# Splitting fp32 values without a mask, with five weight blocks lowered by GpSimd, in a fused two-part model on one core

## The chip, the cores and the metric

The program runs on one core of a Trainium2 chip, in one launch. The metric is the time of the whole program on the device in microseconds. The kernel before was run three times. The profile describes one further execution, of which it gives the span. Engine names are those of the profile: PE is TensorE (PEld its weight loads), DVE is VectorE, ACT is ScalarE, POOL is GpSimd, SP is SyncE, which issues the weight transfers.

## The reference

A sequence of 512 tokens of width 1024 goes through two parts. The first is two layers of this form:

```python
h = rms_norm(x, attn_norm) @ w_in            # 7 full weight blocks and a small one
h = concat(mla(6 heads), diff(6 heads), chunk(4 heads))   # softmax attention
x = x + (out_norms(h) @ w_out)               # 4 weight blocks
h = conv_ffn: rms_norm(x) @ w_ffn_in (1024 x 5632), 3-tap causal convolution over tokens,
x = x + (silu(g) * u) @ w_ffn_out (2816 x 1024)
```

The second part is one layer in which a state-space path (16 groups of states, a complex linear recurrence over the 512 tokens) and a gated attention of its own are mixed, followed by a mixture of 32 experts. All values are float32 and the products are needed nearly at float32 accuracy.

## The kernel before

**Products in three passes.** Activations lie transposed, 128 rows of the model width by 512 tokens to a tile, eight tiles `h[:, k, :]`. TensorE multiplies fp32r operands, which hold fewer bits of the fraction than float32. Each factor is therefore split into a high part in fp32r and a low part, the rest, and a product is three matmuls added into one PSUM bank: high by high, low by high, high by low (L934 to L936 in the two layers, L1178 to L1180 or L1210 to L1212 in the middle stage of the second part, "mid stage" below).

**How a value is split.** In three steps on two engines. DVE masks away the last 12 bits of the fraction (L2190 for weights, L2207 for tiles of `h`, L2502 for weights of the second part). DVE subtracts the masked copy from the source, which gives the low part (L2193, L2210, L2507), and signals `w_lowered` or `h_lowered`. ACT copies the masked part to fp32r (L1686, L1798, L1831, L1901, L1913) and signals `w_split` or `h_split`, on which PE waits.

**Weights** come in blocks of 128 x 2048 words, by one queue of SP, into a ring of three slots (`ring`). The low part of a block is written to `w_low` of its slot, its high part to one of two buffers (`w_high`, `mid_high` in the mid stage).

**Norms.** Before each projection, DVE multiplies tile after tile by the gain and the root (L2217; L2391 after attention), and each finished tile is split at once, one tile behind. ACT computes the root (L1665, L1667). The first PLAIN = 4 matmuls of the accumulation use unsplit values (L954), to give PE something to do before the first split tile is there.

**Attention** is a list of 64 blocks t (diff 0 to 23, chunk 24 to 39, latent "mla" 40 to 63; eight blocks to a pair of heads). For each t, PE makes scores, DVE adds the mask and takes the minimum (an instruction of its own, at L2332 in the kernel after), ACT takes the exponential with its sum (L1765), PE transposes, ACT copies (L1754), PE multiplies with the values. Each engine walks the list in an order written out by hand, each by its own lag.

**The mid stage.** Sixteen state groups st are processed in eight pairs. In pair p PE does, in this order: the input products B (L1241) of its two st, after `z_ready`, the scans of the pair before; a tile of an ordinary projection (128 columns of weights by 512 tokens); the output products C (L1226) of the pair before, after `rotated`; two more tiles. Per st, DVE makes six elementwise operations (L2569 to L2577) and two scans (L2581, `z_ready`), then POOL does four multiplications of 128 x 512 by powers from memory (L1584 to L1587, `rotated`) and loads the next powers (L1572). The projection tiles are `MID_TILES`, two to a weight block b, 15 blocks:

```python
MID_OF_PAIR = [range(0, 2)] + [range(3 * p - 1, min(3 * p + 2, FIRST_QK)) for p in range(1, ST // 2)]
```

ACT copies each finished tile out (L1909, L1926, L1929) and, after every odd tile i, converts block (i + 3) // 2 (L1901). DVE masks and lowers a block between the scans of one st and the elementwise operations of the next.

Of the kernel before, what the change touches and what calls it, by code (L numbers as in the profile page):

```python
# [28 lines left out]
P = 128  # L29
# [18 lines left out]
HIGH_BITS = -(1 << 12)  # L48
# [92 lines left out]
assert 13 + 2 * SMALL.index(("uq", MLA_H - 1)) < FIRST_MLA - 4 and TOKEN_BLOCKS * NQ < 13  # L141

# [144 lines left out]
REST_SPLIT = MID_SPLIT + MID_BLOCKS  # L287
RING0 = LAYERS * LAYER_BLOCKS // RING * 16
# [104 lines left out]
def build(nc, a, out):  # L393
    with ExitStack() as ctx:
# [50 lines left out]
        w_part = [extra[:, 6 * T + n * SLOT:6 * T + (n + 1) * SLOT] for n in range(2)]  # L445
# [9 lines left out]
        h_part = work[:, H_HIGH_AT * T:(H_HIGH_AT + KD) * T].rearrange("p (k t) -> p k t", k=KD)  # L455
# [35 lines left out]
        wf_part = sb("wf_part", [P, 2, KD * FH])  # L491
# [9 lines left out]
        act_part = [work[:, (JF + 6 + n) * T:(JF + 7 + n) * T] for n in range(IN_WORK)] + [spare[:, n, :] for n in range(CH_H)]  # L501
        act_part += tmp[2:4] + [v[:] for v in cmix] + [rt[:, 4 * n:4 * n + 4].rearrange("p a c e -> p (a c e)") for n in range(2)]
        act_part += [rstd[:, 1, :]] + [h_part[:, n, :] for n in range(JF - EARLY)]
# [28 lines left out]
        h2_part = work[:, 0:KD * T].rearrange("p (k t) -> p k t", k=KD)  # L532
        mid_part = [work[:, KD * T + n * SLOT:KD * T + (n + 1) * SLOT] for n in range(2)]
# [10 lines left out]
        h_flat, h_low_flat = h.rearrange("p k t -> p (k t)"), h_low.rearrange("p k t -> p (k t)")  # L544
        w_part.append(h_flat[:, 0:SLOT])
        w_high.append(h_low_flat[:, 0:SLOT])
        part2 = [h_flat[:, 0:SLOT], ys.rearrange("p c t -> p (c t)"), h_flat[:, SLOT:2 * SLOT], extra[:, 0:SLOT]]
        high2 = [h_low_flat[:, 0:SLOT], ys_split, h_low_flat[:, SLOT:2 * SLOT], w2_first[0]]
        for n in range(BLOCKS_OUT2):
            lo = (1 - n % 2) * SLOT  # L550
            part2.append(h_flat[:, lo:lo + SLOT])
            high2.append(h_low_flat[:, lo:lo + SLOT])
        attn_part = extra[:, SLOT:2 * SLOT].rearrange("p (k t) -> p k t", k=4)
# [98 lines left out]
        h_masked = sem("h_masked")  # L652
        h_lowered = sem("h_lowered")
        h_split = sem("h_split")
        w_masked = sem("w_masked")
        w_lowered = sem("w_lowered")
        w_split = sem("w_split")
        act_masked = sem("act_masked")
        act_lowered = sem("act_lowered")
# [240 lines left out]
        def _(pe):  # L900
# [290 lines left out]
            def mid_tile(i):  # L1191
# [3 lines left out]
                if i % 2 == 0:  # L1195
                    pe.wait_ge(w_split, MID_SPLIT + i // 2)
# [92 lines left out]
            for m in range(KD):  # L1289
                n = B2_PSSM + m // 4  # L1290
                pe.wait_ge(w_split, REST_SPLIT + m // 4)
# [43 lines left out]
            for m in range(KD):  # L1335
                n = B2_PATTN + m // 4
                pe.wait_ge(w_split, REST_SPLIT + m // 4 + 2)
# [8 lines left out]
            for m in range(KD):  # L1346
                n = B2_OUT + m // 2
                pe.wait_ge(w_split, REST_SPLIT + m // 2 + 4)
# [154 lines left out]
        def _(pool):  # L1503
# [158 lines left out]
        def _(act):  # L1662
# [18 lines left out]
            for l in range(LAYERS):  # L1681

                def split_high(n, par_, words=SLOT, lo=0):

                    act.wait_ge(w_lowered, n + (l * SPLITS + 1))
                    act.activation(w_high[par_][:, lo:words], w_part[par_][:, lo:words], ACT.Copy).then_inc(w_split, 1)  # L1686

                act.wait_ge(pe_done, done(l, "norm", 0))
                root(l * 2)
                if l == 0:  # L1690
                    split_high(0, 0, lo=PLAIN * 2 * P)
                split_high(1, 1)
                for p, k in enumerate(TILE_ORDER[0]):
                    act.wait_ge(h_lowered, l * (3 * KD) + (p + 1))
                    act.activation(h_high[:, k, :], h_part[:, k, :], ACT.Copy).then_inc(h_split, 1)
# [5 lines left out]
                for t in range(14):  # L1701
# [22 lines left out]
                    if t % 2 and t < 13:  # L1724
                        split_high((t + 3) // 2, (t + 3) // 2 % 2)
# [1425 lines left out]
```

## Time and profile before

| | |
|---|---|
| time, median of 3 runs (lowest to highest) | 2090.63 us (2089.95 to 2091.28) |
| span of the profiled execution | 2087.8 us, 2.8 less than the median |
| PE busy | 1905.3 us, 91% |
| DVE busy | 1278.3 us, 61% |
| ACT busy | 748.9 us, 36% |
| POOL busy | 776.3 us, 37% |
| chain that ended last | PE 77%, DVE 10%, DMA 7%, ACT 4%, issue 2% |

The chain row says which engine's work the end can be followed back through; the 61% of DVE are an average over stages in some of which DVE has no gap at all.

### The profile page before, as it was taken

How to read it: one execution, taken by the hardware profiler on the slowest of the kernel's cores; microseconds unless marked ns; L12 is line 12 of the kernel's file. 1: busy time of each engine (PE TensorE's matmuls, PEld its weight loads, DVE VectorE, ACT ScalarE, POOL GpSimd, SP SyncE). 2: the span in 40 equal slices, each digit the busy share in tenths (PEclk: the TensorE clock that was granted, in tenths of full speed). 3: DMA queues.
4: the chain of work that ended last, by engine and by line, in shares of the span. 5: the costliest groups of instructions: out<-in, count | busy, mean ns of one | idle time of the engine just before them, and what ended most of it. 6: DMA issues, size and time to landing. Idle time of an engine off the chain costs nothing.

```text
span 2087.8 us, 26051 instructions
## 1 busy us (share of the span) xinstructions
PE 1905.3 (91%) x8932; PEld 1344.2 (64%) x8933; DVE 1278.3 (61%) x2070; ACT 748.9 (36%) x1273; POOL 776.3 (37%) x1231
## 2 busy tenths in 40 slices
PE   7998899999999998988999999889999889697784
PEld 5873467888887785456888888666766567333232
DVE  7566667668844637567667864689974885311013
ACT  4256734334422336653334432321225442110000
POOL 0425766676500003676666630065632020111110
PEclk9999999999999999999999999999999998799897
DMA  4210122322233321112323322233322162699995
GB/s 163 91 64 21 61 91 101 111 102 100 96 111 109 127 70 49 41 66 96 111 102 110 105 96 96 108 111 129 105 79 82 41 253 114 234 366 425 421 367 203
DMA packets 42554, 278.11 MB, mean 133 GB/s; under 512 B 7186, under 2 KB 7570, under 8 KB 20560
## 3 DMA queue, kind: packets, MB, share of 16 engines
q1 hardware_dynamic: 31248, 237.66, 30.6%
q0 software_dynamic: 10192, 27.50, 3.6%
q10 hardware_dynamic: 1008, 11.53, 1.4%
q8 instruction: 67, 1.10, 0.2%
q14 instruction: 39, 0.32, 0.0%
HBM read 262.29 MB, written 23.69 MB: 137 GB/s over the span
## 4 chain that ended last, share of the span: by engine, by line
PE 77%; DVE 10%; DMA 7%; ACT 4%; issue 2%; POOL 0%; SPq 0%; ACTq 0%; POOLq 0%; DVEq 0%
PE bank L934 11%; PE bank L935 11%; PE bank L936 11%; DMA all_slots<-in_experts 4%; PE bank L1147 4%; PE bank L1149 4%; PE bank L1148 4%; PE bank L1423 3%; PE bank L1069 2%; PE bank L1083 2%; PE bank L1178 2%; PE bank L1179 2%; PE bank L1180 2%; PE bank L1426 1%; PE bank L1044 1%
## 5 line engine op out<-in xcount | busy, mean ns | idle before, releaser
L934 PE MATMUL bank<-h_high,w_high 128*128 128x512 f32 x1040 | 408.7, 393 | 18.9 <-ACT h_high L1798 12.5
L935 PE MATMUL bank<-h_low,w_high 128*128 128x512 f32 x1040 | 405.9, 390 | 0.0
L936 PE MATMUL bank<-h_high,w_low 128*128 128x512 f32 x1040 | 405.9, 390 | 0.0
L1686 ACT ACTIVATE w_high<-extra 128x2048 fp32r<-128x2048 f32 (+2 forms) x97 | 169.6, 1750 | 284.9 <-DVE w_low L2193 284.8
L2190 DVE TENSOR_SCALAR extra<-ring 128x2048 int32<-128x2048 int32 (+2 forms) x97 | 112.2, 1156 | 211.2 <-PE bank L936 114.8
L934 PEld LDWEIGHTS bank<-h_high,w_high 128*128 128x128 f32 x1040 | 196.0, 188 | 69.3 <-ACT w_high L1686 14.1
L936 PEld LDWEIGHTS bank<-h_high,w_low 128*128 128x128 f32 x1040 | 196.0, 188 | 41.2
L935 PEld LDWEIGHTS bank<-h_low,w_high 128*128 128x128 f32 x1040 | 196.1, 189 | 40.4 <-issue 0.2
L2193 DVE TENSOR_TENSOR w_low<-ring,extra 128x2048 fp32r<-128x2048 f32 (+2 forms) x97 | 204.4, 2107 | 3.3
L1148 PE MATMUL bank<-act_low,w_high 128*128 128x512 f32 x264 | 102.9, 390 | 0.0
L1815 ACT ACTIVATE work<-bank,par 128x512 f32<-128x512 f32 x88 | 66.2, 772 | 76.7 <-PE bank L936 76.7
L1180 PE MATMUL bank<-h_high,w_low 128*128 128x512 f32 x224 | 88.7, 396 | 0.0
L1549 POOL TENSOR_TENSOR work<-work 128x1 f32<-128x1 f32 (+2 forms) x144 | 79.3, 551 | 21.2
L1178 PE MATMUL bank<-h_high,mid_high 128*128 128x512 f32 x208 | 85.3, 410 | 0.4 <-ACT mid_high L1901 0.4
L1179 PE MATMUL bank<-h_low,mid_high 128*128 128x512 f32 x208 | 81.8, 393 | 0.0
L1550 POOL TENSOR_TENSOR work<-work,vpow 128x1 f32<-128x1 f32 (+2 forms) x144 | 74.1, 514 | 20.6
L1551 POOL TENSOR_TENSOR work<-work,vpow 128x1 f32<-128x1 f32 (+2 forms) x144 | 73.6, 511 | 20.6
L1552 POOL TENSOR_TENSOR work<-work 128x1 f32<-128x1 f32 (+2 forms) x144 | 72.4, 502 | 21.4 <-issue 0.3
L1530 POOL TENSOR_SCALAR extra<-extra,stat,lam 128x512 f32<-128x512 f32 (+2 forms) x22 | 21.9, 1004 | 150.8 <-DVE stat L2303 150.8
L1547 POOL TENSOR_TENSOR work<-work,vpow 128x1 f32<-128x1 f32 (+2 forms) x144 | 65.3, 454 | 31.7 <-issue 31.7
L1624 POOL DMA_INDIRECT yrows_d<-ring,scatter_list x14 | 14.2, 1014 | 158.0 <-PE bank L1405 93.9
L2430 DVE SCALAR_TENSOR_TENSOR work<-bank,par,work 128x510 f32<-128x510 f32 x88 | 65.9, 749 | 8.4 <-DVE work L2427 0.6
(584 smaller groups left out, 4091.8 us busy)
## 6 DMA issues: line engine op xcount, KB each, us to landing
all_slots<-in_experts SPq DMA_DIRECT2D x29, 2048.0 KB, 18.2
ring<-in_w_ffn_in SPq DMA_DIRECT2D x44, 1024.0 KB, 4.9
all_slots<-in_experts SPq DMA_DIRECT2D x30, 1024.0 KB, 24.0
ring<-in_w_ffn_out SPq DMA_DIRECT2D x32, 704.0 KB, 4.1
ring<-in_w_feature SPq DMA_DIRECT2D x14, 1024.0 KB, 4.8
ring<-in_w_rest SPq DMA_DIRECT2D x9, 1024.0 KB, 4.9
ring<-in_w_out SPq DMA_DIRECT2D x8, 1024.0 KB, 4.9
powers_d<-work POOLq DMA_DIRECT2D x16, 512.0 KB, 3.4
```

What stands on the lines that cost most here:

```text
L934: pe.matmul(dst, high[:, at], h_high[:, k, :], start=p == 0, stop=False)
L935: pe.matmul(dst, high[:, at], h_low[:, k, :], start=False, stop=False)
L936: return pe.matmul(dst, low[:, at], h_high[:, k, :], start=False, stop=p == KD - 1)
L1147: pe.matmul(dst, high[:, at], act_high[kk], start=kk == 0, stop=False)
L1148: pe.matmul(dst, high[:, at], act_low[:, kk, :], start=False, stop=False)
L1149: ins = pe.matmul(dst, low[:, at], act_high[kk], start=False, stop=kk == JF - 1)
L1178: pe.matmul(dst, high[:, at], h2_high[:, k, :], start=k == 0, stop=False)
L1179: pe.matmul(dst, high[:, at], h_low[:, k, :], start=False, stop=False)
L1180: return pe.matmul(dst, low[:, at], h2_high[:, k, :], start=False, stop=k == KD - 1)
L1686: act.activation(w_high[par_][:, lo:words], w_part[par_][:, lo:words], ACT.Copy).then_inc(w_split, 1)
L2190: dve.tensor_scalar(w_part[par_][:, lo:words].bitcast(I32), ring[slot][:, lo:words].bitcast(I32), HIGH_BITS, None, ALU.bitwise_and).then_i ...
L2193: dve.tensor_tensor(w_low[slot][:, lo:words], ring[slot][:, lo:words], w_part[par_][:, lo:words], ALU.subtract).then_inc(w_lowered, 1)
```

## The change

The mask is gone everywhere. ACT rounds the source itself to fp32r and signals `w_rounded`, `h_rounded` or `act_rounded`. DVE then subtracts the rounded value from the source and signals `w_split` or `h_split`. So the two engines swap order: ACT, which waited for DVE, now waits for the arrival of the weights or for the free buffer, and DVE waits for ACT. Together with it:

- the norm loops lower a tile two steps behind its multiplication, not one;
- the first two of the four `w_out` blocks are split inside the latent attention (rounds after the exponentials of t = 48 and 52, lowers one t later), no longer between attention and the output norm;
- the rounding of the second weight block comes ahead of the root on ACT, in both norms of a layer;
- in the mid stage, blocks 2, 4, 6, 8 and 10 are lowered by POOL, ahead of the multiplications of st = 1, 4, 7, 9 and 12.

```diff
+OUT_WEIGHTS_AT = (FIRST_MLA + 8, FIRST_MLA + 12)
+POOL_MID = {1: 2, 4: 4, 7: 6, 9: 8, 12: 10}
+POOL_BLOCKS = sorted(POOL_MID.values())
...
-                if i % 2 == 0:
-                    pe.wait_ge(w_split, MID_SPLIT + i // 2)
+                if i % 2 == 0 and i // 2 in POOL_BLOCKS:
+                    pe.wait_ge(pool_split, POOL_BLOCKS.index(i // 2) + 1)
+                elif i % 2 == 0:
+                    pe.wait_ge(w_split, MID_SPLIT + dve_mids(i // 2))
...
+            def pool_lower_mid(b):
+                slot = (B2_MID + b) % RING
+                pool.wait_ge(w_rounded, MID_SPLIT + b)
+                pool.tensor_tensor(w_low[slot][:], ring[slot][:], mid_high[b % 2][:], ALU.subtract).then_inc(pool_split, 1)
+
             for st in range(ST):
+                if st in POOL_MID:
+                    pool_lower_mid(POOL_MID[st])
                 pool.wait_ge(z_ready, 2 * (st + 1))
...
-                def split_high(n, par_, words=SLOT, lo=0):
-
-                    act.wait_ge(w_lowered, n + (l * SPLITS + 1))
-                    act.activation(w_high[par_][:, lo:words], w_part[par_][:, lo:words], ACT.Copy).then_inc(w_split, 1)
-
+                def round_weights(n, par_, words=SLOT, lo=0, at=l):
+
+                    act.wait_ge(arrived[n % RING], at * (LAYER_BLOCKS // RING * 16) + 16 * (n // RING + 1))
+                    act.activation(w_high[par_][:, lo:words], ring[n % RING][:, lo:words], ACT.Copy).then_inc(w_rounded, 1)
+
+                if l == 0:
+                    round_weights(0, 0, lo=PLAIN * 2 * P)
+                round_weights(1, 1)
                 act.wait_ge(pe_done, done(l, "norm", 0))
                 root(l * 2)
...
-                split_high(BLOCKS_PROJ, 0)
...
-                split_high(BLOCKS_PROJ + 1, 1)
                 for p, k in enumerate(TILE_ORDER[1]):
-                    act.wait_ge(h_lowered, l * (3 * KD) + (KD + p + 1))
-                    act.activation(h_high[:, k, :], h_part[:, k, :], ACT.Copy).then_inc(h_split, 1)
+                    act.wait_ge(out_normed, l * KD + (p + 1))
+                    act.activation(h_high[:, k, :], h[:, k, :], ACT.Copy).then_inc(h_rounded, 1)
...
+                round_weights(BLOCK_FFN_IN + 1, 1)
                 act.wait_ge(pe_done, done(l, "norm", 1))
                 root(l * 2 + 1)
...
+                    elif t - 1 in OUT_WEIGHTS_AT:
+                        lower_w_out(OUT_WEIGHTS_AT.index(t - 1))
...
             def split_mid(b):
-                if b >= 2:
-                    dve.wait_ge(pe_done, done2(*MID_TILES[2 * b - 3]))
-                mask_block(B2_MID + b, mid_part[b % 2])
-                lower_block(B2_MID + b, mid_part[b % 2], MID_SPLIT + b)
+                if b in POOL_BLOCKS:
+                    return
+                lower_block(B2_MID + b, mid_high[b % 2], MID_SPLIT + b)
```

The wait for the free buffer and for the arrival of a mid block is now ACT's, with the same tile number:

```python
            def mid_weights(b):
                n = B2_MID + b
                if b >= 2:
                    act.wait_ge(pe_done, done2(*MID_TILES[2 * b - 3]))
                act.wait_ge(arrived[n % RING], RING0 + 16 * (n // RING + 1))
                act.activation(mid_high[b % 2][:], ring[n % RING][:], ACT.Copy).then_inc(w_rounded, 1)
```

POOL in the mid stage, before, from the powers load that ends st = 8 to the one that ends st = 9:

```order
L1572 DMA extra<-powers_d 128x1024 [waits rotated]
L1584 TENSOR_TENSOR extra<-extra 128x512 [waits pe_done,powers_in1,z_ready]
L1585 TENSOR_TENSOR extra<-extra 128x512
L1586 TENSOR_TENSOR extra<-extra 128x512
L1587 TENSOR_TENSOR extra<-extra 128x512
L1572 DMA extra<-powers_d 128x1024 [waits rotated]
```

The same place on POOL after the change:

```order
L1570 DMA extra<-powers_d 128x1024 [waits rotated]
L1579 TENSOR_TENSOR w_low<-ring,mid_high 128x2048 [waits w_rounded]
L1589 TENSOR_TENSOR extra<-extra 128x512 [waits pe_done,powers_in1,z_ready]
L1590 TENSOR_TENSOR extra<-extra 128x512
L1591 TENSOR_TENSOR extra<-extra 128x512
L1592 TENSOR_TENSOR extra<-extra 128x512
L1570 DMA extra<-powers_d 128x1024 [waits rotated]
```

The subtraction of block 8, with its wait for ACT's rounding, now stands ahead of the four multiplications of st = 9.

ACT in the mid stage before, from the copies of tiles 10 and 11 to block 9 (the conversions are those of blocks 7, 8 and 9):

```order
L1929 ACTIVATE work<-bank 128x2x256 [waits pe_done] x2
L1901 ACTIVATE mid_high<-work 128x2048 [waits w_lowered]
L1929 ACTIVATE work<-bank 128x2x256 [waits pe_done] x2
L1901 ACTIVATE mid_high<-work 128x2048 [waits w_lowered]
L1905 ACTIVATE rt<-rt 128x512 [waits y_step]
L1926 ACTIVATE work<-bank 128x512 [waits pe_done] x2
L1901 ACTIVATE mid_high<-work 128x2048 [waits w_lowered]
```

And after:

```order
L1935 ACTIVATE work<-bank 128x2x256 [waits pe_done] x2
L1907 ACTIVATE mid_high<-ring 128x2048 [waits arrived0,pe_done]
L1935 ACTIVATE work<-bank 128x2x256 [waits pe_done] x2
L1907 ACTIVATE mid_high<-ring 128x2048 [waits arrived1,pe_done]
L1911 ACTIVATE rt<-rt 128x512 [waits y_step]
L1932 ACTIVATE work<-bank 128x512 [waits pe_done] x2
L1907 ACTIVATE mid_high<-ring 128x2048 [waits arrived2,pe_done]
```

The rows keep their places; what they wait for is a transfer and PE in place of DVE.

ACT in the latent attention after the change, around t = 48 and 52 (L1691 rows are new here; L1759 is the copy, L1770 the exponential):

```order
L1770 ACTIVATE extra,rsum<-extra,stat 128x128 [waits maxed]
L1691 ACTIVATE w_high<-ring 128x2048 [waits arrived0]
L1759 ACTIVATE work<-bank 128x4x128 [waits pe_done]
L1770 ACTIVATE extra,rsum<-extra,stat 128x256 [waits maxed]
L1759 ACTIVATE work<-bank 128x128 [waits pe_done]
L1770 ACTIVATE cmix,rsum<-cmix,stat 128x384 [waits maxed]
L1759 ACTIVATE work<-bank 128x2x128 [waits pe_done]
L1770 ACTIVATE cmix,rsum<-cmix,stat 128x512 [waits maxed]
L1759 ACTIVATE work<-bank 128x3x128 [waits pe_done]
L1770 ACTIVATE rt,rsum<-rt,stat 128x128 [waits maxed]
L1691 ACTIVATE w_high<-ring 128x2048 [waits arrived1]
```

Both roundings of `w_out` blocks fall within one group of eight blocks t; before the change none stands between L1754 and L1765 rows here.

## Rows read from the trace of the kernel before

**Rows 1.** The page: span, busy times, chain that ended last

```profile
span 2087.8 us, 26051 instructions
...
PE 1905.3 (91%) x8932; PEld 1344.2 (64%) x8933; DVE 1278.3 (61%) x2070; ACT 748.9 (36%) x1273; POOL 776.3 (37%) x1231
...
PE 77%; DVE 10%; DMA 7%; ACT 4%; issue 2%; POOL 0%; SPq 0%; ACTq 0%; POOLq 0%; DVEq 0%
```

**Rows 2.** Groups by line: xcount | busy, mean ns | idle before, releaser

```profile
L1686 ACT ACTIVATE w_high<-extra 128x2048 fp32r<-128x2048 f32 (+2 forms) x97 | 169.6, 1750 | 284.9 <-DVE w_low L2193 284.8
L2190 DVE TENSOR_SCALAR extra<-ring 128x2048 int32<-128x2048 int32 (+2 forms) x97 | 112.2, 1156 | 211.2 <-PE bank L936 114.8
...
L2193 DVE TENSOR_TENSOR w_low<-ring,extra 128x2048 fp32r<-128x2048 f32 (+2 forms) x97 | 204.4, 2107 | 3.3
```

**Rows 3.** Waits of PE: us in total, times, longest

```profile
PE bank L934 <- ACT h_high L1798: 12.5, 2, 6.3
...
PE bank L934 <- ACT h_high L1831: 5.5, 5, 1.3
...
PE bank L1241 <- DVE extra L2581: 4.9, 1, 4.9
...
PE bank L1332 <- ACT extra L2006: 3.1, 2, 2.4
```

**Rows 4.** Windows: stretch, length, busy by engine, granted clock

```profile
core 0: us, PE busy (x) PEld busy (x) DVE busy (x) ACT busy (x) POOL busy (x), PEclk, DMA share, GB/s
213.44:223.31 9.87, 9.87 (x54) 5.18 (x53) 5.00 (x24) 7.15 (x23) 7.69 (x8) 1.00 0.10 44
...
1380.00:1500.00 120.00, 120.00 (x597) 84.20 (x594) 111.74 (x111) 26.16 (x26) 77.74 (x54) 0.97 0.32 106
1376.30:1386.50 10.20, 7.25 (x16) 3.99 (x17) 10.13 (x11) 2.87 (x2) 8.37 (x6) 0.50 0.35 138
```

**Rows 5.** Timeline of DVE, ffn norm of layer 0: start, us, instruction

```profile
313.40 0.96 DVE L2207 TENSOR_SCALAR work<-h 128x512 int32<-128x512 int32 x1
314.40 0.98 DVE L2210 TENSOR_TENSOR h_low<-h,work 128x512 fp32r<-128x512 f32 x1
315.31 1.10 DVE L2217 SCALAR_TENSOR_TENSOR h<-x,par,rstd 128x512 f32<-128x512 f32 x1
...
317.92 0.74 DVE L2217 SCALAR_TENSOR_TENSOR h<-x,par,rstd 128x512 f32<-128x512 f32 x1
318.58 0.42 DVE L2207 TENSOR_SCALAR work<-h 128x512 int32<-128x512 int32 x1
319.04 0.69 DVE L2210 TENSOR_TENSOR h_low<-h,work 128x512 fp32r<-128x512 f32 x1
```

**Rows 6.** Timeline of ACT and PE, output norm of layer 0

```profile
253.88 1.93 ACT L1686 ACTIVATE w_high<-extra 128x2048 fp32r<-128x2048 f32 x1
...
256.47 0.77 PE L934 MATMUL bank<-h_high,w_high 128*128 128x512 f32 x1 [6.22 <-ACT h_high L1798]
```

**Rows 7.** Timeline of DVE, POOL and PE, first pair of the mid stage

```profile
1369.97 3.27 DVE L2507 TENSOR_TENSOR w_low<-ring,work 128x2048 fp32r<-128x2048 f32 x1
...
1371.05 3.34 POOL L1585 TENSOR_TENSOR extra<-extra 128x512 f32<-128x512 f32 x1
1374.35 1.27 POOL L1586 TENSOR_TENSOR extra<-extra 128x512 f32<-128x512 f32 x1
...
1376.86 2.33 DVE L2581 TENSOR_TENSOR_SCAN extra<-s,extra 128x512 f32<-128x512 f32 x2
...
1379.24 1.22 PE L1241 MATMUL bank<-work,extra 32*128 32x512 f32 x2 [4.93 <-DVE extra L2581]
```

**Rows 8.** Timeline of ACT, POOL and PE, sixth pair

```profile
1472.95 0.60 ACT L1929 ACTIVATE work<-bank 128x512 f32<-128x512 f32 x1 [5.16 <-PE bank L1212]
...
1472.93 1.72 POOL L1587 TENSOR_TENSOR extra<-extra 128x512 f32<-128x512 f32 x1
...
1480.44 1.05 PE L1226 MATMUL bank<-extra,cmix 128*32 128x512 f32 x4
```

More of the change, by code:

```diff
@@ L287, with dve_mids @@
 REST_SPLIT = MID_SPLIT + MID_BLOCKS
+POOL_MID = {1: 2, 4: 4, 7: 6, 9: 8, 12: 10}
+POOL_BLOCKS = sorted(POOL_MID.values())
+def dve_mids(b):
+    return sum(n not in POOL_BLOCKS for n in range(b))
 RING0 = LAYERS * LAYER_BLOCKS // RING * 16
@@ L1826, in conv_g @@
                     return par[:, bass.ds(j + lo, 1)]
-                split_high(SPLIT_FFN + 1, 1)
                 for p, k in enumerate(TILE_ORDER[2]):
-                    act.wait_ge(h_lowered, l * (3 * KD) + (2 * KD + p + 1))
-                    act.activation(h_high[:, k, :], h_part[:, k, :], ACT.Copy).then_inc(h_split, 1)
-                for j in range(2):
-                    conv_tap(j, j, done(l, "ffn_in", j, 0), None)
-                    split_high(SPLIT_FFN + j + 2, j)
-                    silu(j, l * (2 * JF) + 2 * (j + 1))
@@ L1836, in _ @@
-                with act.Fori(1, LOOPED // 2) as r:
-                    for s in range(2):
-                        j = r * 2 + s
-                        conv_tap(j, s, r * 4 + (done(l, "ffn_in", s, 0)), r * 2 + (l * JF + (s - 1)))
-                        split_high(j + (SPLIT_FFN + 2), s)
-                        silu(s, r * 4 + (l * (2 * JF) + 2 * (s + 1)))
+                    act.wait_ge(normed, l * (2 * KD) + (KD + k + 1))
+                    act.activation(h_high[:, k, :], h[:, k, :], ACT.Copy).then_inc(h_rounded, 1)
@@ L2015, in _ @@
                     turn2(u - LAG2)
[L2016 removed]
+                if u == PATTN_SPLIT:
                     weight_high2(2)
@@ L2037, in _ @@
             for k in range(KD):
-                tile_high2(MIXED_SPLIT + k + 1, mixed_both[:, KD + k, :], gates[:, KD + k, :])
-                if k == 2:
+                act.wait_ge(mixed, k + 1)
+                act.activation(mixed_both[:, KD + k, :], gates[:, k, :], ACT.Copy).then_inc(h_rounded, 1)
+                if k == 3:
                     weight_high2(4)
@@ L2214, in normalise_and_split @@
                     dve.wait_ge(rstd_ready, l * 2 + (norm + 1))
-                    for k in range(KD + 1):
+                    for k in range(KD + 2):
                         if k < KD:
@@ L2551, in _ @@
             dve.wait_ge(final_step, 2)
-            for k in range(KD + 1):
+            for k in range(KD + 2):
                 if k < KD:
```

322 lines of the change are left out of this document (136 added, 186 removed).

## The prediction

> **What bounds the kernel now.** I read the page first. PE is busy 91% of a span of 2087.8 us [rows 1], so the change can only help where PE waits, and hurts where it makes PE wait. DVE looks relieved most: by line, 97 masks of weights cost it 112.2 us beside the 204.4 of the subtractions [rows 2]. How little of that is on PE's path shows in the list of what PE waited for [rows 3]: 12.5 us in two waits for the first split tile after the output norms, 5.5 for later tiles of the ffn norms, one wait of 4.9 for a scan. Next the windows [rows 4]: over 120 us of the mid stage PE has no gap at all although DVE is busy 111.74, and in a group of eight blocks of the latent attention PE is full while ACT works 7.15 of 9.87 us and DVE 5.00. In such stretches work taken from DVE is worth nothing, and what is added can open a gap. Last the timelines at the norms and in the mid stage [rows 5 to 8]. Two things are to be seen there. A POOL multiplication of 128 x 512 takes 1.27 us alone and 3.34 when it overlaps a DVE subtraction that itself takes 3.27 [rows 7]: the two engines take turns. And a short idle time on PE is followed by a granted clock of 0.50, the lower level of 1.2 GHz, for some 10 us [rows 4], in which PE does half.
>
> **The change, part by part.** Signs are of the end: plus is later.
>
> *Start.* ACT now rounds the second weight block ahead of the root, 1.75 us on the mean [rows 2], and waits for its arrival; PE's unsplit matmuls cover most: +0.3, bounds 0 and +1.8.
>
> *Tiles at the norms.* DVE spends on a tile of the ffn norm 0.74 + 0.42 + 0.69 = 1.85 us, and 0.96 + 0.98 + 1.10 = 3.04 where POOL's squares run beside it [rows 5]. Without the mask it is 1.43 and 2.08. So I take 0.35 for each of four tiles (PE's own time for a tile, 1.4, is the floor) and 0.96 for each of two: 3.3. The multiplications start 0.7 later, because DVE's second weight subtraction waits for ACT's rounding. Layer 0: -2.6. Layer 1 read in the same way -1.9, its attention norm -0.7, the last norm -0.4: -5.6 in all. Bounds: -2 (the tile two behind waits for ACT each time) and -8.
>
> *Output norm.* Before the first `w_out` matmul ACT has a weight conversion of 1.93 that ends at 255.8, and PE waits until 256.47 [rows 6]. Two conversions and four DVE instructions leave this place. The first tile is then bound by DVE: root, multiplication, subtraction, some 1.4 earlier; part goes back because PE starts at the low clock, where its first matmul takes 0.77 [rows 6]. -1.0 in each layer, -2 in all; bounds 0 and -5.
>
> *Where they went.* Two roundings of 1.93 [rows 6] now fall on ACT in t = 48 to 55: 7.15 + 3.86 = 11.0 us in a period of 9.87 [rows 4]. The excess of 1.1 has to come out of PE, unless the neighbouring periods, with 2.7 of slack each, take it. But ACT walks in order: behind a rounding stand the copy and the exponential for which PE's transposes wait a few blocks later, and on DVE the reciprocal and the minimum of the next block stand behind the subtraction. Going through the lags by hand, the block after the first rounding is some 1.9 late for PE, after the second 0.5. I take +2.2 a layer, +4.4 in all, bounds 0 and +3 a layer.
>
> *Mid stage, POOL's five subtractions.* The trace has no 128 x 2048 subtraction on POOL. From below: DVE does one in 2.1 us [rows 2]. From above: four times 1.27 [rows 7], 5.1. I take 4.7, since a fixed share of the 1.27 is paid once. The Trainium skill, "GPSIMD Engine Reference", section "Performance versus the Vector engine", gives 4.5 us for such an operation of 2048 elements in fp32; by it each term below would be 0.2 less.
>
> The place that decides is block 8, ahead of the multiplications of st = 9. POOL must wait for ACT's rounding, and that for the end of tile 13, which PE makes in the fifth pair and which ends at 1472.8, where ACT's copy begins [rows 8]. Copy 0.6, semaphores 0.1, rounding 1.9: 1475.4. Subtraction 4.7: 1480.1. Four multiplications of 1.27: 1485.2. In the trace the multiplications of st = 9 end at 1472.93 + 1.72 = 1474.65, and PE comes to the output products that need them at 1480.44 [rows 8]. So PE waits at least 4.8 us there. In these 10 us DVE lowers and has six elementwise operations and two scans of 2.33 to run [rows 7]; by the rule of turns they stretch POOL by some 2.7: 7.5. After such a gap the clock falls. Around the wait for the scan PE was busy 7.25 us at a granted clock of 0.50 [rows 4], which did the work of 3.6 and so cost 3.6; I take 2.5, as this gap is preceded by dense work. Block 8: +10.
>
> Block 2 stands ahead of st = 1 on POOL. ACT, which no longer waits for DVE, rounds it from 1374 (the copy of tile 1) to 1376, POOL subtracts from there to 1380.7, and the scans of st = 1, which began at 1376.86 [rows 7] and for which PE waited already 4.9 us [rows 3], either run beside it or after it. By turns they end at 1383 rather than at 1379.2, the start of PE's B products being 1379.24: +4.3; without turns 0. Blocks 4, 6 and 10 leave POOL late by 1.0, 0.3 and 1.0 for PE in the same bookkeeping. Mid stage: +16.6. Bounds: +2.5 (a subtraction as fast as DVE's, no taking of turns) and +22 (5.1 each, twice the clock loss).
>
> Here the taking of turns is the disputed step. What the rows show is 3.34 for 1.27 [rows 7]. The Trainium skill, "SBUF — State Buffer", section "Who interferes with whom", says that a DVE operation with two inputs in SBUF and a GpSimd operation that reads SBUF exclude one another for the whole instruction, whoever is first; so a 4.7 us subtraction holds DVE's next two-input operation back by up to 4.7. Trace and rule agree on the short ones. Without the rule, with bare durations alone, the mid stage would be +4.8 and some clock.
>
> *After the mid stage.* DVE loses eight more masks of weights and those of 20 tiles. PE waits in the second attention for ACT, 3.1 us at one line [rows 3], and elsewhere under 3 for both. I take -3, bounds 0 and -6. In the ffn stages PE is dense, and rounding first or last is the same for it: 0.
>
> **Sum.** 0.3 - 5.6 - 2 + 4.4 + 16.6 - 3 = +10.7 on the profiled 2087.8, which gives 2098.5; that execution is 2.8 under the median, whose scale gives 2101.3. I say 2100.
>
> **Rivals.**
> *Slower by the stall of block 8 (forecast)*, chance 0.6: 2095 to 2108. For it: the chain of rows 8 has no free term, each microsecond of POOL's subtraction is one of PE.
> *The subtractions cost only their bare length*, chance 0.17: DVE and POOL run side by side, block 2 costs nothing, block 8 4.8 and no more. Sum 0.3 - 5.6 - 2 + 4.4 - 3 + 4.8 = -1.1: 2089.5, no change. Against it stands the 3.34 of rows 7.
> *Faster*, chance 0.2: the mid stage hides what POOL does. Place: the output products after st = 9. POOL would do 2048 columns in 2.1 us, as DVE does; then block 8 costs 2.2. With the rest at -5.9 this is -3.7, 2087; the sign turns to faster by more than 0.2% where the mid stage costs less than 1.7, or less than 6 if ACT's slack also covers the latent attention (-10.3 for the rest), which gives 2083 to 2086. For it: ACT is the least busy engine. Against it: no POOL row runs at DVE's speed.
> *Much slower*, chance 0.03: the late POOL does not catch up, since it is busy 77.74 of 120 us and now has 23 more [rows 4], and each pair is bound by POOL: above 2108.
>
> **Numbers.** A measurement of this kernel can tell about 0.2%, 4 us. The first case lies above 2095 nearly throughout; the bare-length case is split, most of it within 4 us; the third is mostly faster. That makes faster 0.19, same 0.17, slower 0.64. The range goes from the third case's 2086 to 2108. The likeliest case's own range is 2095 to 2108.
>
> **What would show it.** In the changed profile: a wait of PE at the output products (L1224) for POOL, of 5 to 9 us, and none such elsewhere in the mid stage beyond 2; POOL's subtraction at 4.5 to 5.1 us; the wait for the scan before the second pair at 8 to 9 us instead of 4.9; a granted clock of 0.50 after both; tiles of the ffn norm 1.4 apart; the first `w_out` matmul after the output norm about 1 us sooner; small waits of PE in the latent attention of each layer, near t = 47 to 52. The prediction is wrong if POOL's subtractions are much shorter, if DVE's scans run through beside them, or if the norms give back more than 8.

## The result, and the profile after

The changed kernel takes 2117.1 us in the median (2115.12 to 2117.92), the kernel before 2090.95 in the same series. The ratio is 1.012, with a 95% interval of 1.0107 to 1.0132: slower, as forecast, but by 26 us where 10.7 were worked out, and above the range. The profiled execution has a span of 2115.9 us, 28.1 more than that of [rows 1]. The kernel before itself lies anywhere from about 2089 to 2097 us, at mean granted clocks of 0.969 to 0.965, so that its median moved by 3 us between the series of this document with nothing changed. The page of the changed kernel, against [rows 1]:

```profile
span 2115.9 us, 25647 instructions
...
PE 1914.9 (90%) x8932; PEld 1354.0 (64%) x8933; DVE 1065.6 (50%) x1820; ACT 736.9 (35%) x1273; POOL 723.0 (34%) x1236
...
PE 79%; DMA 7%; DVE 6%; ACT 4%; issue 3%; POOL 1%; SPq 0%; ACTq 0%; POOLq 0%; DVEq 0%
```

DVE has lost 213 us of work and POOL has not grown, and yet the program is longer. What PE waited for, against [rows 3] (us in total, times, longest):

```profile
PE bank L950 <- DVE h L2215: 15.0, 4, 5.0
PE bank L1239 <- DVE extra L2556: 13.4, 2, 9.8
PE bank L930 <- DVE h_low L2208: 9.4, 2, 4.7
...
PE bank L1224 <- POOL extra L1592: 7.8, 2, 6.8
...
PE bank L1079 <- ACT work L1759: 4.3, 4, 1.5
...
PE bank L1065 <- ACT work L1759: 3.4, 2, 1.7
...
PE bank L1065 <- DVE extra L2311: 1.8, 2, 0.9
```

L930 is the first `w_out` matmul: two waits of 4.7 where there were two of about 6.2. L1239 is the wait for a scan, 4.9 once before and now 9.8 and 3.5; L1224, for POOL, is new, with one wait of 6.8 and one of 1.1; L1079 and L1065 for ACT are the latent attention, whose group of [rows 4] had no gap. The waits of 0.9 for L2311, one in each layer, are new too and come early in the attention.

Both kernels issue the same 8932 matmuls, so the start of a matmul after, less its start before, shows where time is lost. This shift is +1.5 us at the start of the latent attention of layer 0 (0.9 of it by the wait for L2311) and +4.9 at its end, +3.4 at the first `w_out` matmul, +3.8 at the end of that projection, +6.2 at the end of the unsplit matmuls of the ffn norm and +2.8 after its tiles. Layer 1 goes much the same way, and the shift is +1.4 after the last norm. Then come +6.3 ahead of st = 2, +7.0 after the products behind it, +14.8 after the products that follow st = 8, +24.0 after the output products of st 8 and 9, +24.5 at the end of the mid stage, and +27.8 where the experts begin. So 23 of the 28 us are the mid stage's.

The second pair of the mid stage, DVE, POOL and PE, against [rows 7]:

```profile
1379.11 6.37 DVE L2556 TENSOR_TENSOR_SCAN extra<-s,extra 128x512 f32<-128x512 f32 x2
...
1378.77 4.51 POOL L1579 TENSOR_TENSOR w_low<-ring,mid_high 128x2048 fp32r<-128x2048 f32 x1
...
1385.54 3.78 PE L1239 MATMUL bank<-work,extra 32*128 32x512 f32 x8 [9.85 <-DVE extra L2556]
```

Two scans that took 2.33 take 6.37: POOL's subtraction of block 2 began 0.3 us ahead of them. (x2 means that the row merges two instructions: the first scan took 5.26, the second 1.19.) The same again at block 6, ahead of st = 8, where the kernel before has no gap:

```profile
1454.65 4.56 POOL L1579 TENSOR_TENSOR w_low<-ring,mid_high 128x2048 fp32r<-128x2048 f32 x1
...
1454.74 5.57 DVE L2556 TENSOR_TENSOR_SCAN extra<-s,extra 128x512 f32<-128x512 f32 x1
...
1460.36 3.78 PE L1239 MATMUL bank<-work,extra 32*128 32x512 f32 x8 [3.54 <-DVE extra L2556]
```

The subtraction came 0.09 us before the second scan of st = 7. And block 8, against [rows 8]:

```profile
1488.22 1.90 ACT L1907 ACTIVATE mid_high<-ring 128x2048 fp32r<-128x2048 f32 x1
...
1490.21 4.62 POOL L1579 TENSOR_TENSOR w_low<-ring,mid_high 128x2048 fp32r<-128x2048 f32 x1 [7.21 <-ACT mid_high L1907]
1494.81 2.17 POOL L1589 TENSOR_TENSOR extra<-extra 128x512 f32<-128x512 f32 x1
...
1502.06 1.07 PE L1224 MATMUL bank<-extra,cmix 128*32 128x512 f32 x2 [6.76 <-POOL extra L1592]
```

That is the chain of the forecast, link by link. The windows behind the three waits show what each costs besides:

```profile
core 0: us, PE busy (x) PEld busy (x) DVE busy (x) ACT busy (x) POOL busy (x), PEclk, DMA share, GB/s
1385.54:1395.00 9.46, 9.46 (x23) 5.74 (x24) 5.51 (x8) 0.00 (x0) 5.54 (x5) 0.54 0.18 57
1458.80:1469.00 10.20, 8.64 (x31) 6.11 (x32) 6.20 (x8) 0.00 (x0) 5.96 (x6) 0.52 0.17 51
1500.20:1507.00 6.80, 4.95 (x12) 1.10 (x14) 0.50 (x1) 0.00 (x0) 2.40 (x3) 0.50 0.26 81
```

The last two begin shortly before the end of the wait (at 1460.36 and 1502.06). Where PE is busy in the three, it runs at or near half the clock. Behind st = 8 the shift goes from 10.6 to 14.8 without an idle moment: a wait of 3.5 cost 7.8. Behind the wait of 1.1, at 1570.22, the granted clock stayed at 1.00 and nothing more was lost.

### The profile page after: what moved, and what is told of

It reads as the page before. It is cut to its first block, busy times and chain, and to the rows that moved or that the text cites. A ratio compares the mean times of both kernels' runs of the same rounds, so it can differ in the third digit from the quotient of the medians.

```text
span 2115.9 us, 25647 instructions
## 1 busy us (share of the span) xinstructions
PE 1914.9 (90%) x8932; PEld 1354.0 (64%) x8933; DVE 1065.6 (50%) x1820; ACT 736.9 (35%) x1273; POOL 723.0 (34%) x1236
## 4 chain that ended last, share of the span: by engine, by line
PE 79%; DMA 7%; DVE 6%; ACT 4%; issue 3%; POOL 1%; SPq 0%; ACTq 0%; POOLq 0%; DVEq 0%
PE bank L930 11%; PE bank L932 11%; PE bank L931 11%; DMA all_slots<-in_experts 4%; PE bank L1143 4%; PE bank L1145 4%; PE bank L1144 4%; PE bank L1421 3%; PE bank L1079 2%; PE bank L1065 2%; PE bank L1174 2%; PE bank L1175 2%; PE bank L1176 2%; PE bank L1424 1%; PE bank L1283 1%
## 5 line engine op out<-in xcount | busy, mean ns | idle before, releaser
L930 PE MATMUL bank<-h_high,w_high 128*128 128x512 f32 x1040 | 409.1, 393 | 9.8 <-DVE h_low L2208 9.4
L2197 DVE TENSOR_TENSOR w_low<-ring,w_high 128x2048 fp32r<-128x2048 f32 (+2 forms) x97 | 202.7, 2090 | 329.1 <-ACT w_high L1691 329.1
L930 PEld LDWEIGHTS bank<-h_high,w_high 128*128 128x128 f32 x1040 | 196.5, 189 | 54.1 <-issue 13.4
L1691 ACT ACTIVATE w_high<-ring 128x2048 fp32r<-128x2048 f32 (+2 forms) x97 | 168.7, 1740 | 143.2 <-PE bank L1145 102.3
L1826 ACT ACTIVATE work<-work 128x512 f32<-128x512 f32 x44 | 27.8, 632 | 233.4 <-DVE work L2422 233.4
L1548 POOL TENSOR_TENSOR work<-work,vpow 128x1 f32<-128x1 f32 (+2 forms) x144 | 70.6, 490 | 20.6
L1547 POOL TENSOR_TENSOR work<-work 128x1 f32<-128x1 f32 (+2 forms) x144 | 64.9, 451 | 21.2
L1550 POOL TENSOR_TENSOR work<-work 128x1 f32<-128x1 f32 (+2 forms) x144 | 64.0, 445 | 21.4 <-issue 0.5
L1421 PE MATMUL bank<-all_slots,tail 128*32 128x512 f32 x384 | 50.6, 687 | 19.9 <-DMA all_slots<-in_experts 19.9
L1549 POOL TENSOR_TENSOR work<-work,vpow 128x1 f32<-128x1 f32 (+2 forms) x144 | 60.4, 419 | 20.6
```

The costliest lines, as they stand in the source:

```text
L930: pe.matmul(dst, high[:, at], h_high[:, k, :], start=p == 0, stop=False)
L1421: ins = pe.matmul(b[s * ROWS:(s + 1) * ROWS, :], xt[:, k * P + s * ROWS:k * P + (s + 1) * ROWS], expert_part(first + s, k * 2 * DE, 2 * DE ...
L1691: act.activation(w_high[par_][:, lo:words], ring[n % RING][:, lo:words], ACT.Copy).then_inc(w_rounded, 1)
L2197: dve.tensor_tensor(w_low[slot][:, lo:words], ring[slot][:, lo:words], w_high[par_][:, lo:words], ALU.subtract).then_inc(w_split, 1)
```

## The experiments

Theory A says that POOL's five subtractions make the mid stage's 23 us, by holding DVE's scans and by the chain of block 8. The rival is that ACT's place ahead of DVE in the split makes the blocks late. For the 5 us outside the mid stage there are theories C to G, told with their runs. The kernel before ran along in each series, at medians of 2090.95 to 2094.03. Kernels of different series are compared by their medians, and a difference of a few us between them is uncertain by some 2 us; what the ratios to the kernel before give is named where it differs. Where it matters I go by the shifts between traces as well, and a trace is one execution.

**All mid blocks on DVE.**

```diff
-POOL_MID = {1: 2, 4: 4, 7: 6, 9: 8, 12: 10}
+POOL_MID = {}
```

> All 15 mid-stage blocks are lowered by DVE again (nothing else differs from the changed kernel at 2117.1 us). Theory A, the five subtractions on POOL cost the mid stage its 23 us: the waits of 9.85 (second pair, scan), 3.54 (scan before st = 8), 6.76 (output products of st 8 and 9) and 1.08 us go back to one wait of about 5, the clock stays high after st = 8, and the time is 2095 (2093 to 2098). Rival B, the mid stage is late because ACT's rounding now comes ahead of DVE's subtraction and waits for a finished tile: waits of 3 to 7 us stay, 2105 to 2117.

2095.04 us, ratio to before 1.0011 (1.0001 to 1.0021). One wait for a scan is left, 5.8, and none for POOL. Theory A holds: 22.1 of the 26 us are POOL's subtractions, and the rival falls. The shift says the same: in this trace it is +2.4 where the mid stage begins and +2.3 where it ends. The wait ahead of st = 2 is still 0.9 longer than before the change; that part is not POOL's. All else in the change comes to no gain.

**Block 8 one st later.**

```diff
-POOL_MID = {1: 2, 4: 4, 7: 6, 9: 8, 12: 10}
+POOL_MID = {1: 2, 4: 4, 7: 6, 10: 8, 12: 10}
```

> Only block 8's subtraction moves on POOL, from ahead of the multiplications of st = 9 to ahead of those of st = 10. Theory A, a fixed chain (tile 13, copy, rounding, subtraction, four multiplications) is late for the output products of st 8 and 9: their wait of 6.76 and the 2.6 lost to the low clock behind it go, 2108 (2106 to 2110). Rival B, POOL as a whole is the bound of the pairs by now: the wait moves to the next output products, 2115 to 2118.

2108.11 us (ratio 1.0077, 1.0058 to 1.0095). The wait of 6.76 is gone, the one of 1.1 for st 12 and 13 is left. The chain of block 8 was worth 9.0 (9.3 by the shift in the change), and POOL as a whole is not the bound. The wait for the scan before st = 8 is as in the change, 3.55, but the clock behind it cost 3.1 here where it cost 4.1 there.

**Block 6 on DVE.**

```diff
-POOL_MID = {1: 2, 4: 4, 7: 6, 9: 8, 12: 10}
+POOL_MID = {1: 2, 4: 4, 9: 8, 12: 10}
```

> Block 6 goes back to DVE, the other four stay on POOL. Theory A, its 4.56 us subtraction held the scan of st = 7 (5.57 us instead of 1.2) and the low clock came behind it: the wait of 3.54 ahead of st = 8 and some 4.5 of clock go, 2109 (2107 to 2111). Rival B, the lateness would have come with the output products of st 8 and 9 anyway, whose wait grows by what is saved here: 2114 to 2118.

2109.13 us (ratio 1.0077, 1.0058 to 1.0096). The waits are 9.8 for the scan and 6.8 for POOL, as in the change; only the one of 3.5 and the clock behind it are gone, 8.0 us (9 by the ratios, 7.8 by the shift in the change). Block 2 had no run of its own; by the shifts it cost 5.7 in the change, against 0.7 with all blocks on DVE, so 5.0. With 9.0 for block 8 the three come to 22.0, and the costs add.

**Each subtraction in four pieces.**

```diff
-                pool.tensor_tensor(w_low[slot][:], ring[slot][:], mid_high[b % 2][:], ALU.subtract).then_inc(pool_split, 1)
+                for q in range(4):
+                    lo = q * T
+                    ins = pool.tensor_tensor(w_low[slot][:, lo:lo + T], ring[slot][:, lo:lo + T], mid_high[b % 2][:, lo:lo + T], ALU.subtract)
+                ins.then_inc(pool_split, 1)
```

> Each POOL subtraction of 128x2048 is issued as four of 128x512, in the same place. Theory A, DVE and POOL exclude one another for the length of one instruction: a scan waits for one quarter (1.3 us) and not for the whole, so the scan of st = 7 falls from 5.57 to 2.5 or less, the wait of 3.54 goes to about 1 and the one of 9.85 to about 8, while block 8's chain stretches by 1 to 2: 2108 to 2114. Rival B, POOL is late by its total work, whatever the pieces: unchanged or, by four fixed costs, slower, 2117 to 2121.

2116.53 us (ratio 1.0121, 1.01 to 1.0142). DVE and POOL in this kernel, at block 2 and block 6:

```profile
1379.61 6.78 DVE L2559 TENSOR_TENSOR_SCAN extra<-s,extra 128x512 f32<-128x512 f32 x2
...
1454.37 4.63 DVE L2559 TENSOR_TENSOR_SCAN extra<-s,extra 128x512 f32<-128x512 f32 x2
```

```profile
1379.27 4.92 POOL L1581 TENSOR_TENSOR w_low<-ring,mid_high 128x512 fp32r<-128x512 f32 x4
...
1456.60 5.91 POOL L1581 TENSOR_TENSOR w_low<-ring,mid_high 128x512 fp32r<-128x512 f32 x4
```

The two scans of st = 7 are merged in the row of block 6. The second of them and the first piece, alone:

```profile
1456.60 1.30 POOL L1581 TENSOR_TENSOR w_low<-ring,mid_high 128x512 fp32r<-128x512 f32 x1
...
1456.69 2.31 DVE L2559 TENSOR_TENSOR_SCAN extra<-s,extra 128x512 f32<-128x512 f32 x1
```

Half a confirmation. At block 6 the first piece came 0.09 us before the scan, as the whole subtraction had in the change, and the scan took 2.31 and not 5.57: it waited for one piece and went ahead of the second. PE's wait fell from 3.54 to 1.21, as theory A has it. At block 2 the expectation failed: the four pieces ran in a row in 4.92 and the scans took 6.78, so no scan got in between two pieces, and the wait was 10.2. By the shifts the mid stage lost 18.9 us where it had lost 23.1, with longer waits for POOL at block 8 and block 10 (7.2 and 2.0); the medians do not show a gain. Pieces are no sure remedy. The next two runs put the question about the exclusion in another way.

**POOL only writes, or reads half.** In place of the subtraction, one memset of the block's low part; and a memset of one half with a subtraction of the other. The first leaves out the low part of the five blocks, the second half of it.

```diff
-                pool.tensor_tensor(w_low[slot][:], ring[slot][:], mid_high[b % 2][:], ALU.subtract).then_inc(pool_split, 1)
+                for q in range(1):
+                    ins = pool.memset(w_low[slot][:].bitcast(F32), 0.0)
+                ins.then_inc(pool_split, 1)
```

> The changed kernel with each of POOL's five subtractions replaced by one memset of the same 128x2048 place (the low parts of blocks 2, 4, 6, 8 and 10 are left out, so this kernel computes less). The memset only writes and should last some 2 us. If the exclusion is one of reading (The Trainium skill, SBUF — State Buffer, Who interferes with whom, says so), the scans of st = 1 and 7 take their 2.33 for two beside it, and the waits ahead of st = 2 and 8 are those of mid_dve (5.8 and none). If any operation of POOL holds DVE back, a scan beside the memset takes about 3 and the first wait is 7 to 8.

2101.71 us (ratio 1.0046, 1.0031 to 1.006).

```profile
1379.11 2.33 DVE L2558 TENSOR_TENSOR_SCAN extra<-s,extra 128x512 f32<-128x512 f32 x2
...
1378.74 1.82 POOL L1580 MEMSET w_low<- 128x2048 f32 x1
...
1381.50 3.78 PE L1239 MATMUL bank<-work,extra 32*128 32x512 f32 x8 [5.80 <-DVE extra L2558]
```

```diff
-                pool.tensor_tensor(w_low[slot][:], ring[slot][:], mid_high[b % 2][:], ALU.subtract).then_inc(pool_split, 1)
+                pool.memset(w_low[slot][:, 2 * T:].bitcast(F32), 0.0)
+                pool.tensor_tensor(w_low[slot][:, 0:2 * T], ring[slot][:, 0:2 * T], mid_high[b % 2][:, 0:2 * T], ALU.subtract).then_inc(pool_split, 1)
```

> As write_only, but POOL memsets one half of the block and subtracts the other half (128x1024), so it reads for some 2.3 us (half of the low part of the five blocks is left out). If the reading instruction holds DVE's two-input scan for its own length, one scan takes up to 2.3 + 1.2 = 3.5 us, half of what the change showed (5.57), and the wait ahead of st = 2 lies midway, at 7 to 8. If the scans were late for another reason (ACT's rounding, the powers), they are as in the change, 5.3 to 5.6 for one.

2106.18 us (ratio 1.0073, 1.0058 to 1.0089).

```profile
1379.64 4.43 DVE L2557 TENSOR_TENSOR_SCAN extra<-s,extra 128x512 f32<-128x512 f32 x2
...
1380.19 2.80 POOL L1580 TENSOR_TENSOR w_low<-ring,mid_high 128x1024 fp32r<-128x1024 f32 x1
...
1384.12 3.78 PE L1239 MATMUL bank<-work,extra 32*128 32x512 f32 x8 [7.91 <-DVE extra L2557]
```

The memset began 0.37 us ahead of the scans, where the subtraction had been 0.34 ahead, and the scans took their 2.33. In the second kernel the half subtraction began beside the first scan, which took its 1.21, and the second scan took 3.29: together 4.43. Beside the whole one they took 6.37. So a scan is held by POOL's reading instruction that is ahead of it, until that ends. "SBUF — State Buffer" of the Trainium skill, section "Who interferes with whom", says this in one rule: a GpSimd instruction that only writes SBUF does not disturb a DVE instruction with two inputs there, one that reads does. The traces agree. DVE's six elementwise operations of an st have one input in PSUM and keep their 0.67 to 0.70 us beside POOL, beside a whole subtraction too (that of block 2 in blocks_later, 1386.45 to 1391.07). The wait of PE at the output products of st 8 and 9 was 3.53, 5.54 and 6.76 in the three kernels, where POOL spends 1.80, 3.35 and 4.62 on block 8: about 1.1 per microsecond, as a chain without slack has it.

**The same blocks on POOL, later.**

```diff
-POOL_MID = {1: 2, 4: 4, 7: 6, 9: 8, 12: 10}
+POOL_MID = {2: 2, 4: 4, 8: 6, 10: 8, 12: 10}
```

> POOL lowers the same five blocks as in the change, but blocks 2, 6 and 8 one st later (ahead of st = 2, 8 and 10). Theory A: the collision with the scans of st = 1 (4.9 us), with the scan of st = 7 (3.5 and the clock behind it) and the late output products of st 8 and 9 all go, 2095 to 2099, as with all blocks on DVE. Rival: the collisions only move to the next scans, 2103 to 2112.

2098.2 us (ratio 1.003, 1.002 to 1.004): one wait of 1.1 for POOL is left, and the wait for the first scan is 5.8. The place was the cost, not POOL's share of the work; but nothing is won by that share. The collisions have not gone: the first scans of st = 2, 8 and 10 take 3.97, 5.07 and 4.00. PE did not wait for them. It waits for both st of a pair, and blocks 2, 6 and 8 now stand ahead of the first st of a pair, with the second still to come; in the change they stood ahead of the second.

**The two w_out roundings apart** (on the base of all mid blocks on DVE).

```diff
-OUT_WEIGHTS_AT = (FIRST_MLA + 8, FIRST_MLA + 12)
+OUT_WEIGHTS_AT = (FIRST_MLA + 4, FIRST_MLA + 14)
```

> All mid blocks on DVE, and the roundings of the first two w_out blocks moved from t = 48 and 52 to t = 44 and 54, so that each falls into another group of eight latent blocks. Theory C, as forecast: two roundings overfill ACT's period of 9.87 us, one fits (7.15 + 1.93 = 9.08): the waits of 1.68 and 1.48 in each layer go, 2089 (2087 to 2091). Rival D: each insertion stops the chain of minimum and exponential by itself, because DVE waits for the rounding and then subtracts (4.2 us in series): still about 3.4 a layer, 2094 to 2096.

2088.72 us (ratio 0.9987, 0.9978 to 0.9997), 6.3 below its base, 5.0 by the ratios. Waits at L1065 of 1.68 and at L1079 of 1.48 go in each layer, and two of 0.87 and 0.89 take their place elsewhere. By the shifts the latent attention costs 2.2 a layer here and 3.45 in the base, so 1.3 a layer are gained in it. The rest of the 6.3 lies in the projection and the ffn norm behind it, which the edit does not touch and where the low clock is shorter in this trace; whether that follows from the edit is not shown.

**The subtraction three blocks later** (same base).

```diff
-                    elif t - 1 in OUT_WEIGHTS_AT:
-                        lower_w_out(OUT_WEIGHTS_AT.index(t - 1))
+                    elif t - 3 in OUT_WEIGHTS_AT:
+                        lower_w_out(OUT_WEIGHTS_AT.index(t - 3))
```

> All mid blocks on DVE, roundings at t = 48 and 52 as in the change, but DVE lowers three t later instead of one, when the rounding is long done. Theory C (ACT's period is overfull): hardly anything, 2093 to 2096. Rival D (DVE's wait for the rounding, in series with its subtraction, holds the minimum that the next exponential needs): the waits of 1.68 and 1.48 fall to under 0.5 each, 2089 (2088 to 2092).

2097.92 us (ratio 1.0024, 1.0014 to 1.0034), 2.9 above its base, against the forecast of theory D. DVE no longer stands still for the rounding, and the wait of 1.68 at L1065 is gone in each layer; but that at L1079 grows from 1.48 to 2.82. The idle time of a layer is thus a little less than in the base, 2.8 for 3.2. What makes it slower is the clock: from 227.70 to 234.50 the granted clock is 0.50 here, and in the base it is 1.00 all through this place; the latent attention costs 5.7 a layer. So this run settles neither theory. It shows that one wait of 2.8 was dearer than two of 1.68 and 1.48. Why the second wait grew was only read, not tried: the second subtraction now begins 3.6 us after the start of its rounding, between an exponential and the next minimum.

**The second ffn weight block behind the tiles** (same base).

```diff
-                round_weights(BLOCK_FFN_IN + 1, 1)
                 act.wait_ge(pe_done, done(l, "norm", 1))
                 root(l * 2 + 1)
+                round_weights(BLOCK_FFN_IN + 1, 1)
...
-                lower_in(1, 1)
                 normalise_and_split(1, 2, lambda k: g("ffn_norm", k))
+                lower_in(1, 1)
```

> All mid blocks on DVE, and in the ffn norm the second weight block is rounded by ACT behind the root and lowered by DVE behind the tiles. Theory E: the subtraction of this block ahead of the first multiplication costs its start 0.7 and, through a longer stretch at the low clock, 1.7 more: the ffn norms of both layers get 1.5 to 2.5 shorter each, 2091 (2089 to 2093). Rival F: the start is set by the root and the block was never on the path: unchanged, 2094 to 2096.

2091.25 us (ratio 0.9995, 0.9986 to 1.0005), 3.8 below its base, 3.3 by the ratios. By the shifts the ffn norms get 0.9 (layer 0) and 2.0 (layer 1) shorter than in the base, so theory E holds, on the evidence of the medians and of one pair of traces, and the same move at the attention norm, below, bears it out; the fall of the waits at L950, by 1.3 to 12.2, is small beside their spread among the kernels with no edit there (13.2 to 15.0). The low clock at this place is no sign of it: it was granted for 6.8 us in the change (312.3 to 319.1), for 3.4 in the kernel before, and for 3.4 (314.1 to 317.5) in the base of this run, whose code here is that of the change.

**Put together.** The edits of the last three that helped (all mid blocks on DVE, roundings at t = 44 and 54, second ffn block behind the tiles).

> The three places put right together: mid blocks all on DVE, roundings of w_out at t = 44 and 54, second ffn weight block behind the root and the tiles. If their costs add (22.1, 6.3 and 3.8 us), 2117.1 - 32.2 = 2085 (2083 to 2087), which is also what the forecast gave for the change without its costs. Rival: spreading and the later block earn partly the same low clock, 2087 to 2089.

2085.36 us (ratio 0.9967, 0.9957 to 0.9978). The costs add, as well as medians of different series can tell: 2117.1 - 32.2 = 2084.9.

In addition, the same for the attention norm:

```diff
-                round_weights(1, 1)
                 act.wait_ge(pe_done, done(l, "norm", 0))
                 root(l * 2)
+                round_weights(1, 1)
...
-                lower_proj(1)
                 dve.wait_ge(par_in, l * 16 + 16)
                 normalise_and_split(0, 0, lambda k: g("attn_norm", k))
+                lower_proj(1)
```

> As three_undone, and the second weight block of the attention norm goes behind the root and the tiles too. Theory E (a subtraction ahead of the first multiplication is on the path) gives 1 to 2 us in the two layers, 2083 to 2084. Rival: at this norm the rounding waits for nothing and the root is later anyway, 2085 to 2086.

2084.31 us (ratio 0.9954, 0.994 to 0.9969). A gain of 1.0 in the medians is within what the intervals leave open. The trace shows more at the place itself: the first matmuls of layer 0 are through 4.1 earlier than in three_undone, the attention norm of layer 1 gives back another 2.2, and the waits at L950 fall from 12.9 to 9.4. In this execution, the slowest of the five, about 3 of that are lost again at other places; the run of all four, below, keeps the gain.

Or, with POOL at the later places:

```diff
-POOL_MID = {}
+POOL_MID = {2: 2, 4: 4, 8: 6, 10: 8, 12: 10}
```

> As three_undone, but POOL lowers five mid blocks, at the later places (ahead of st = 2, 4, 8, 10 and 12). If DVE's relief in the mid stage is worth nothing, because PE has no gap there, this is not faster than three_undone: 2085 to 2088, with one wait of about 1 for POOL. If it is worth something: under 2084.

2089.01 us (ratio 0.9984, 0.9973 to 0.9994), slower than without by 3.7 in the medians, 2.9 in the spans. Apart from the wait of 5.8 ahead of st = 2, which is the same in both, PE has no gap in the mid stage that a less busy DVE could close.

Or, with one subtraction later in the last projection of attention:

```diff
-                if m_ == 3:
+                if m_ == 4:
                     lower_weights2(4)
```

> As three_undone, but in the last projection of attention DVE subtracts weight block 4 one step later (m = 4). Theory G: there DVE stands still for ACT's rounding and then subtracts, which gave the wait of 2.57 at the seventh tile (1.53 before the change); it falls below 1 and the time is 1 to 3 us below three_undone, 2082 to 2084. Rival: the wait is POOL's and ACT's chain of the mixed tiles, unchanged.

2082.16 us (ratio 0.9955, 0.9941 to 0.9969), 3.2 below three_undone, and 2.6 by the shift over the stage. The wait of 2.57 at the projection matmuls (L1283, for L2686) is gone, 0.4 is left. Theory G holds: in the change ACT's rounding of 1.90 and DVE's subtraction of 2.29 stood in series (1726.16 to 1730.38) ahead of the multiplication that empties the bank PE waits for.

**All four.**

> All four places put right in one kernel: mid blocks on DVE, roundings of w_out spread to t = 44 and 54, the second weight block behind the root and the tiles in both norms of a layer, block 4 of the last projections one step later. If the gains of 1.0 and 3.2 over three_undone add: 2081 (2079 to 2083), 0.6% below the kernel before. Rival: they overlap, 2082 to 2084.

2078.4 us (ratio 0.9938, 0.9926 to 0.9951), which is 12.6 below the kernel before and 38.7 below the change. It gave more than the sum of 1.0 and 3.2. Against three_undone_l4, which lacks only the edit of the attention norm, it is 3.8 faster in the medians and 3.9 by the shift, with 4.3 gained at the start of layer 0 and some of it lost again: so this edit is worth about 4 and not 1.0.

## Why the prediction was wrong

The sign and its main reason were right, the size was not.

- **Block 8: right.** "So PE waits at least 4.8 us there", 7.5 taken: 6.76. With the clock, +10 forecast, +9.3 by the shift and 9.0 by its own run. A subtraction of 4.7 was taken; it takes 4.51 to 4.62, close also to the 4.5 that the Trainium skill, "GPSIMD Engine Reference", section "Performance versus the Vector engine", gives for an addition of this size.
- **Block 2: right in kind, with some luck.** +4.3 forecast for the scans of st = 1; the wait grew by 4.9, but 0.9 of that is there with all blocks on DVE too, and the clock behind it added 0.7. The +4.3 does not come out of its own sentence either: scans that end at 1383 and not at 1379.2 give 3.8.
- **Block 6: the step that failed.** "Blocks 4, 6 and 10 leave POOL late by 1.0, 0.3 and 1.0". Only POOL's own lateness was counted, 0.3 for block 6. Its subtraction came 0.09 us ahead of the second scan of st = 7 and held it to its end: 3.5 us of wait and 4.1 to 4.5 of low clock, 7.8 by the shift and 8.0 by its own run. The rule for this was in the text and applied to block 2. Where a long reading instruction of POOL is free to drift along a row of DVE's, the bound has to hold a collision with each of them. The upper bound of +22 for the mid stage did not, and 22.1 by the medians, 23.1 by the shift, is what was measured.
- **The clock behind a short wait.** 2.5 was taken for block 8 and nothing for block 6. It cost 2.4 behind 6.76, 4.1 behind 3.54 (3.1 in block8_later, behind 3.55) and nothing behind 1.1. In these rows the longer wait does not have the higher price; what sets it is not shown.
- **After the mid stage: wrong sign.** -3 forecast, +3.4 measured. Masks taken from DVE were counted and the new wait of DVE for ACT was not. At the seventh tile of the last projection PE's wait is 2.57 for 1.53 before, and moving one subtraction gave 3.2 back, 2.6 by the shift.
- **Latent attention: mis-sized.** +2.2 a layer, bound +3; the shift is +3.45 a layer. The reason given (11.0 us of ACT in 9.87) is right in part: with one rounding to a period 2.2 a layer are still lost. How much of that is DVE's standing still and how much the order of ACT's work stays open.
- **Norms: mis-sized.** "-5.6 in all" came to -4.4 by the shifts. Layer 0 gave -1.0 for -2.6: the tiles gave what was said, 3.4 by the shift, at 1.27 us a tile on DVE, but the unsplit matmuls lost 2.4, under a low clock of 6.8 us. In the trace of mid_dve, with the same code here, the low clock was 3.4 us and this norm gave the -2.6 of the forecast, so the miss is one of the execution and not of the reasoning. Layer 1 gave -2.4 for -1.9, its attention norm +0.6 for -0.7, and the last norm -1.7 for -0.4.
- **Output norm: right in kind.** -1.0 a layer; the wait fell from 6.2 to 4.7. The projection behind it then lost 0.4 and 1.2.

The shifts account for the whole difference. The mid stage is +23.1 for +16.6, what follows it +3.4 for -3, the latent attention +6.9 for +4.4, the norms -4.4 for -5.6 and the start +0.6 for +0.3: 16.9 more than forecast. The output norms took back 1.1. Three terms were not in the forecast at all: +1.8 for the two waits for L2311, +1.6 in the projections behind the output norms, and -2.0 in the ffn. That leaves 17.2, and 17.4 is what the difference of the spans, 28.1, exceeds the sum of 10.7 by.

## What to carry to other kernels

When a step is turned round between two engines (round first, subtract after), list for each place what now stands behind the engine that must wait; here that ate every microsecond that the saved masks gave, until four places were put right one by one. Later is not always better: in the latent attention the later subtraction was slower. Work given to an idle POOL is cheap only where nothing waits for the two-input instructions from SBUF that DVE has due during it, and where no chain without slack runs through it; in such a chain PE paid about its whole length. And each new gap is to be priced with the clock behind it, here 2.4 to 4.1 us behind waits of 3.5 to 6.8, and nothing behind 1.1.

## What was not expected of the hardware

- A POOL memset of 128x2048 takes 1.80 to 1.82 us and leaves a two-input scan beside it at 1.21; a POOL subtraction of the same size takes 4.51 to 4.62, and a scan that came just behind it took 5.26 or 5.57.
- Four POOL subtractions of 128x512 issued in a row took 4.92 us while a DVE scan waited, and kept it out. In the same execution, at block 6, a scan got in behind the first of four. What decides this stays open.
- A wait of PE of 3.54 us was followed by 8.6 us (1460.36 to 1469.00) at a granted clock of 0.50, one of 6.76 by 4.9 us (1502.06 to 1507.00): much of the second stretch of low clock fell into the wait itself.
- With nothing changed at a place, the stretch of low clock there was 3.4 us in one trace and 6.8 in another (the ffn norm of layer 0, in mid_dve and in the change).
